# A transformer kernel on one Trainium2 core: modulation weights through the weight ring in three groups, feed-forward residual added on VectorE

## What is computed

```python
x = x + gla_mixer(rms_norm(x, norm1))
x = x + conv_ffn(rms_norm(x, norm2), w_up, conv_w, conv_b, w_down)
x = rms_norm(x, final_norm)

mod = silu(c) @ w_ada + b_ada                  # 1024 x 6144
sh1, sc1, gt1, sh2, sc2, gt2 = split(mod, 6)
h = x * (1.0 + sc1) + sh1
y = token_mixer(h, ...)
x = layer_norm(alpha * x + (1.0 + gt1) * y, ...)
h = x * (1.0 + sc2) + sh2
y = hier_moe(h, ...)                           # 32 experts, 2 per token
x = layer_norm(alpha * x + (1.0 + gt2) * y, ...)
```

## Time and profile before

| | |
|---|---|
| runs | 1503.31, 1504.61, 1504.91 us |
| profiled execution: its own time | 1502.36 us |
| its span, first to last instruction | 1500.6 us |
| mean granted TensorE clock | 0.929 |
| busy: TensorE / VectorE / ScalarE | 1238.5 / 382.4 / 248.2 us |
| moved by DMA | 332.73 MB, mean 222 GB/s |

### The profile page before, as it was taken

One profiled execution on the slowest core, in us unless ns is written; L12 is line 12 of the kernel. 1 busy time (PEld: TensorE's weight loads), 2 busy tenths in 40 slices (PEclk: granted clock), 3 DMA queues, 4 the chain that ended last, 5 costly groups with the idle time before them and its releaser, 6 DMA issues.

```text
span 1500.6 us, 21760 instructions
## 1 busy us (share of the span) xinstructions
PE 1238.5 (83%) x8810; PEld 855.2 (57%) x8811; DVE 382.4 (25%) x898; ACT 248.2 (17%) x519; POOL 31.9 (2%) x12
## 2 busy tenths in 40 slices
PE   6997899999969999999799999577757547776773
PEld 4644477777747778878579886343323224443331
DVE  1103121121121714332524211422211121222123
ACT  1311011111110111352121100211111111111112
POOL 0000000000000000000322000000000000000000
PEclk9999999999998999999999899879988889988787
DMA  8442366766722354233030046659999999899993
GB/s 302 160 144 86 119 199 225 260 199 228 253 105 84 102 207 154 73 138 126 19 113 1 1 151 220 224 203 395 393 394 395 393 394 395 305 393 393 396 393 135
DMA packets 184258, 332.73 MB, mean 222 GB/s; under 512 B 8961, under 2 KB 55169, under 8 KB 184082
## 3 DMA queue, kind: packets, MB, share of 16 engines
q1 hardware_dynamic: 184210, 332.04, 61.3%
HBM read 330.97 MB, written 1.05 MB: 221 GB/s over the span
## 4 chain that ended last, share of the span: by engine, by line
PE 65%; SPq 18%; DMA 5%; DVE 5%; ACT 3%; issue 3%; PEldq 1%; PEld 1%; DVEq 0%; ACTq 0%
SPq L428 18%; PE ps L481 17%; PE ps L598 10%; PE ps L489 9%; PE ps L607 5%; DMA main<-in_w_up 4%; PE ps L998 3%; PE ps L616 2%; PE ps L863 1%; PE ps L868 1%; PE ps L988 1%; PE ps L1013 1%; PE ps L867 1%; PE ps L768 1%; PE ps L473 1%
## 5 line engine op out<-in xcount | busy, mean ns | idle before, releaser
L998 PE MATMUL ps<-main 128*32 128x256 f32 x2176 | 165.8, 470 | 144.4 <-DMA main<-in_w_up 116.8
L481 PE MATMUL ps<-main 128*128 128x256 f32 x1152 | 252.6, 381 | 1.3 <-DVE main L1345 1.3
L481 PEld LDWEIGHTS ps<-main 128*128 128x128 f32 x1152 | 219.4, 191 | 33.9 <-issue 2.6
L998 PEld LDWEIGHTS ps<-main 128*32 128x32 f32 x2176 | 84.9, 134 | 225.4 <-DMA main<-in_w_up 126.5
L598 PE MATMUL ps<-main 128*128 128x256 f32 x704 | 155.4, 379 | 0.0
L598 PEld LDWEIGHTS ps<-main 128*128 128x128 f32 x704 | 133.0, 190 | 25.2 <-issue 8.1
L489 PE MATMUL ps<-main 128*128 128x512 f32 x320 | 138.3, 593 | 4.3 <-DVE main L1577 2.6
L489 PEld LDWEIGHTS ps<-main 128*128 128x128 f32 x320 | 60.5, 190 | 79.6 <-issue 74.6
L1406 DVE SCALAR_TENSOR_TENSOR main<-ps,cols,main 128x255 f32<-128x255 f32 (+1 forms) x88 | 38.4, 478 | 188.1 <-ACT main L1129 185.2
L1771 DVE TENSOR_TENSOR main<-main,ps 64x256 f32<-64x256 f32 x34 | 14.4, 423 | 270.8 <-ACT main L1286 270.8
L607 PE MATMUL ps<-main 128*128 128x512 f32 x176 | 81.0, 603 | 0.0
(11 more groups left out here) (307 smaller groups left out, 1095.2 us busy)
## 6 DMA issues: line engine op xcount, KB each, us to landing
main<-in_w_up SPq DMA_DIRECT2D x32, 2048.0 KB, 22.1
main<-in_w_down SPq DMA_DIRECT2D x32, 2048.0 KB, 19.5
main<-in_w_gate SPq DMA_DIRECT2D x32, 2048.0 KB, 19.1
main<-in_w_in SPq DMA_DIRECT2D x15, 2048.0 KB, 7.6
main<-in_w_ada SPq DMA_DIRECT2D x12, 2048.0 KB, 9.6
main<-in_l_ffn_w_up SPq DMA_DIRECT2D x44, 512.0 KB, 5.2
main<-in_l_gla_w_in SPq DMA_DIRECT2D x6, 2048.0 KB, 13.1
main<-in_l_ffn_w_down SPq DMA_DIRECT2D x22, 512.0 KB, 6.8
```

Source lines behind the costliest of these rows:

```text
L481: m = pe.matmul(ps[:, banks[m4 // 2], (m4 % 2) * T:(m4 % 2) * T + T], chunk8(n)[:, k, m4 * P:(m4 + 1) * P], act[:, k, :], start=(k == 0), ...
L998: m = pe.matmul(ps[q * SLOTS:(q + 1) * SLOTS, 5, 0:T], xsel[s][:, k, :], w, start=(k == 0), stop=(k == KD - 1))
```

## The change

`w_ada`'s 12 chunks become ring chunks, in three groups of four. Group 0 takes numbers 6 to 9, the output projection 10 and 11 (`C_GO`), groups 1 and 2 numbers 12 to 19; the second block begins at 20. Group 0's matmuls stand between the attention's last matmul and the transposes of its output, group 1's between the output projection and the transposes of the second norm, group 2's between the last `ff_down` and the third norm's transposes. A group fills one PSUM bank, ScalarE copies it as a whole (`take_ada`), TensorE transposes it in four pieces, VectorE adds bias and, where needed, 1, in two operations. The feed-forward loses the modulation work and the matmuls with the identity; its first `ff_down` starts the sum, and VectorE adds x at the end. The silu of the condition moves to the beginning.

```diff
         for i in range(6):
             add_chunk(wide(w_gla, HALF * i))
-        for i in range(2):
-            add_chunk(wide(I["l0_gla_w_out"], HALF * i))
+        C_ADA = [add_ada(0)]
+        C_GO = [add_chunk(wide(I["l0_gla_w_out"], HALF * i)) for i in range(2)]
+        C_ADA += [add_ada(1), add_ada(2)]
         N_FIRST = len(CHUNKS)
...
-            for n in range(N_FIRST):
+            for n in range(6):
                 load_ring(sp, n)
...
-            sp.wait_ge(S["y_turned"], 4)
-            load_ada(0)
-            for n in range(N_FIRST, N_FIRST + RING):
+            for n in range(6, N_FIRST):
                 load_ring(sp, n)
             with sp.Fori(1, FT // 2) as i:
 
                 load_up(i * 2, 0, i * 2 - 1)
                 load_up(i * 2 + 1, 1, i * 2)
-                load_ada(i, i)
                 load_down(i * 2, 0, i * 2 - 1)
                 load_down(i * 2 + 1, 1, i * 2)
-            load_ada(11, 11)
...
-            for n in range(N_FIRST + RING, N_SECOND):
+            for n in range(N_FIRST, N_SECOND):
                 load_ring(sp, n)
...
+            def ada(group, b):
+
+                for a, n in enumerate(C_ADA[group]):
+                    ring_wait(pe, n)
+                    for k in range(KD):
+                        for q in range(4):
+                            m = pe.matmul(ps[q * 32:(q + 1) * 32, b, a * P:(a + 1) * P], cond[:, k:k + 1].broadcast_to([P, 32]),
+                                          chunk8(n)[:, k, q * P:(q + 1) * P], start=(k == 0), stop=(k == KD - 1), skip_group_check=True)
+                    m.then_inc(S["chunk_done"], 1)
+
+            def ada_turn(group, b):
+
+                pe.wait_ge(S["ada_rows_ready"], group + 1)
+                for a in range(4):
+                    m = pe.transpose(ps[:, b, a * P:(a + 1) * P], ada_rows[:, a * P:(a + 1) * P], ident)
+                m.then_inc(S["ada_turned"], 1)
+
+            pe.wait_ge(S["cond_ready"], 1)
+            ada(0, 6)
             pe.wait_ge(S["y_ready"], 2)
+            pe.wait_ge(S["ada_rows_ready"], 1)
             turn_rows(y_rows, (0, 1, 5, 6), "y_turned")
...
+            ada_turn(0, 1)
+            ada(1, 0)
             pe.wait_ge(S["rows_scaled"], 4)
             turn_rows(xn, (4, 5, 6, 7), "turned")
-            for j in range(NT):
-                for half in range(2):
-                    pe.matmul(ps[:, 2 * j + half, :], ident, x[:, j, half * HALF:(half + 1) * HALF], start=True, stop=False)
             pe.wait_ge(S["turned_copied"], 8)
...
             ff_up(0, 0, (None,))
             ff_up(1, 1, (None,))
-            pe.wait_ge(S["cond_ready"], 1)
-            ada(16)
-            ff_down(1, 16, 0)
-            ada_turn(1)
+            ada_turn(1, 7)
+            pe.wait_ge(S["mod_ready"], 1)
+            ff_down(1, 16, 0, first=True)
             with pe.Fori(1, FT // 2) as i:
                 ff_up(i * 2, 0, (i * 2 - 1, i * 32 + 32))
                 ff_down(i * 2, i * 16, 1)
                 ff_up(i * 2 + 1, 1, (i * 2, i * 32 + 32))
-                ada(i * 16 + 16)
                 ff_down(i * 2 + 1, i * 16 + 16, 0)
-                ada_turn(i + 1, i)
-            ada(16 * 12)
             ff_down(FT, 16 * (FT // 2), 1, last=True)
-            ada_turn(12, 11)
+            ada(2, 6)
...
+            pe.wait_ge(S["ada_rows_ready"], 3)
             turn_k(x, "x_turned")
...
             m.then_inc(S["chunk_done"], 1)
+            ada_turn(2, 3)
             ring_wait(pe, C_KW)
...
             norm_root(0, [x[:, j, :] for j in range(NT)], NT)
+            act.wait_ge(S["cols_loaded"], 16)
+            act.activation(cond, col("cond"), ACT.Silu).then_inc(S["cond_ready"], 1)
...
+            def take_ada(group, b):
+
+                act.wait_ge(S["chunk_done"], C_ADA[group][3] + 1)
+                if group:
+                    act.wait_ge(S["ada_turned"], group)
+                act.activation(ada_rows, bank(b), ACT.Copy).then_inc(S["ada_rows_ready"], 1)
...
+            modulation(0, 1, 0)
+            ff_conv(0, 0, 0, 2)
+            ff_mul(0, 0, None)
+            modulation(1, 7, 8)
...
-                    if s == 0:
-                        modulation(i - 1, i)
-                take_ada(i + 1)
-            modulation(10, 11)
-            take_ada(12)
-            modulation(11, 12)
             dve.wait_ge(S["down_done"], FT)
-            dve.tensor_copy(unit(0), bank(0, 4)).then_inc(S["x2_ready"], 1)
+            dve.tensor_tensor(unit(0), unit(0), bank(0, 4), ALU.add).then_inc(S["x2_ready"], 1)
...
-            dve.wait_ge(S["mod_ready"], 12)
-            dve.tensor_scalar(mod[:, 8:24], mod[:, 8:24], 1.0, None, ALU.add).then_inc(S["mod_plus"], 1)
-            dve.tensor_scalar(mod[:, 32:48], mod[:, 32:48], 1.0, None, ALU.add).then_inc(S["mod_plus"], 1)
-            dve.wait_ge(S["mod_plus"], 2)
+            dve.wait_ge(S["mod_ready"], 2)
...
```

More of the change, by code:

```diff
@@ L176, in build_program, with add_ada @@
         w_gla = I["l0_gla_w_in"]
+        w_ada = I["w_ada_2"].rearrange("b d n -> (b d) n")
+        def add_ada(group):
+            return [add_chunk(wide(w_ada, HALF * (4 * group + i))) for i in range(4)]
         for i in range(6):
             add_chunk(wide(w_gla, HALF * i))
-        for i in range(2):
-            add_chunk(wide(I["l0_gla_w_out"], HALF * i))
+        C_ADA = [add_ada(0)]
+        C_GO = [add_chunk(wide(I["l0_gla_w_out"], HALF * i)) for i in range(2)]
+        C_ADA += [add_ada(1), add_ada(2)]
         N_FIRST = len(CHUNKS)
@@ L241, in build_program @@
         ident = const("ident")
[L245 to L246 removed]
+        ada_rows = unit(10, 0, HALF)
         mod = small[:, 32:80]
@@ L600, in ff_up, with ff_down @@
                 m.then_inc(S["up_done"], 1)
-            def ff_down(done, loaded, s, last=False):
+            def ff_down(done, loaded, s, first=False, last=False):
                 pe.wait_ge(S["hm_ready"], done)
@@ L607, in ff_down @@
                         m = pe.matmul(ps[:, 2 * j + half, :], hm[s][:, j * P:(j + 1) * P],
-                                      down_w[s][:, half * HALF:(half + 1) * HALF], start=False, stop=last)
+                                      down_w[s][:, half * HALF:(half + 1) * HALF], start=first, stop=last)
                 m.then_inc(S["down_done"], 1)
[L611 to L625, removed]
             ff_up(0, 0, (None,))
             ff_up(1, 1, (None,))
-            pe.wait_ge(S["cond_ready"], 1)
-            ada(16)
-            ff_down(1, 16, 0)
-            ada_turn(1)
+            ada_turn(1, 7)
+            pe.wait_ge(S["mod_ready"], 1)
+            ff_down(1, 16, 0, first=True)
             with pe.Fori(1, FT // 2) as i:
@@ L687, in _ @@
             pe.wait_ge(S["widx_ready"], 1)
+            pe.wait_ge(S["mod_ready"], 3)
             project_cols(C_QA[0], (2, 3), act=h1T)
@@ L1142, in _ @@
             norm_root(3, [x[:, j, :] for j in range(NT)], NT)
-            act.wait_ge(S["mod_plus"], 2)
+            take_ada(2, 6)
+            act.wait_ge(S["mod_ready"], 2)
             for k in range(4):
@@ L1392, in _ @@
             for half, banks in ((0, (2, 4)), (1, (3, 7))):
-                dve.wait_ge(S["chunk_done"], 7 + half)
+                dve.wait_ge(S["chunk_done"], C_GO[half] + 1)
                 for j in range(NT):
@@ L1419, in ff_mul, with modulation @@
                 dve.tensor_tensor(hm[s], sig[s], conv[s][:, 1, :], ALU.mult).then_inc(S["hm_ready"], 1)
-            def take_ada(done):
-                dve.wait_ge(S["ada_done"], done)
-                dve.tensor_copy(ada_rows, ps[:, 6, 0:P]).then_inc(S["ada_rows_ready"], 1)
-            def modulation(i, done):
-                dve.wait_ge(S["ada_turned"], done)
-                dve.tensor_tensor(mod[:, bass.ds(i * 4, 4)], ps[:, 7, 0:P].rearrange("p (q r) -> p q r", q=4)[:, :, 0], cols[:, bass.ds(COLS["b_ada"][0] + i * 4, 4)], ALU.add).then_inc(S["mod_ready"], 1)
-            for i in range(2):
-                ff_conv(i, i, i, 2 * i + 2)
-                ff_mul(i, i, None)
-            take_ada(1)
+            def modulation(group, b, plain):
+                dve.wait_ge(S["ada_turned"], group + 1)
+                turned = bank(b).rearrange("p (n r) -> p n r", n=16)[:, :, 0]
+                bias = col("b_ada")[:, 16 * group:16 * group + 16]
+                for n0 in (0, 8):
+                    m = dve.scalar_tensor_tensor(out=mod[:, 16 * group + n0:16 * group + n0 + 8], in0=turned[:, n0:n0 + 8],
+                                                 scalar=0.0 if n0 == plain else 1.0, in1=bias[:, n0:n0 + 8], op0=ALU.add, op1=ALU.add)
+                m.then_inc(S["mod_ready"], 1)
+            modulation(0, 1, 0)
+            ff_conv(0, 0, 0, 2)
+            ff_mul(0, 0, None)
+            modulation(1, 7, 8)
+            ff_conv(1, 1, 1, 4)
+            ff_mul(1, 1, None)
             with dve.Fori(1, FT // 2) as i:
@@ L1465, in _ @@
             dve.tensor_scalar(widx, ps[:, 2, 0:2 * IH], INDEX_SCALE, None, ALU.mult).then_inc(S["widx_ready"], 1)
```

(1 more changed line is left out.)

16 lines of the change are left out of this document (8 added, 8 removed).

## The result

| | before | after |
|---|---|---|
| median | 1504.76 us (1503.31 to 1505.05, 4 runs) | 1599.43 us (1599.06 to 1602.31, 4 runs) |
| ratio, 95% interval | | 1.0635 [1.0617, 1.0654] |
| span of the profiled execution | 1500.6 us | 1597.3 us |
| mean granted clock | 0.929 | 0.899 |

The kernel became 6.4% slower: 94.7 us, where 32.5 us of gain were predicted. TensorE's busy time hardly changed (1238.5 before, 1253.5 after), so the loss is waiting. The question is where.

What follows compares the result with a forecast made beforehand. TensorE was taken to bound the feed-forward, with everything behind moving along. Residual add 30.0 us earlier, plus 3.1 of clock, minus 0.5 for transposes, taken as 32.5: profiled 1502.36 to 1469.9, median 1472.1 us, range 1467 to 1482.

Steps and rivals of the forecast that it cites:

- First norm: Before the attention's output projection: group 0's chunks fill TensorE's idle time at full clock; projection ends 0.6 us earlier.
- Second norm: Before the feed-forward: group 1's fourth chunk lands late, a 1.5 us wait; up projections still start 2.0 us earlier.
- Entry: Into the feed-forward loop: up weights queue behind chunks 16 to 19, 0.5 us stall; loop starts at 199.55, 2.9 earlier.
- the case of late weights: Rival, chance 0.12: loads behind the second norm come later than counted, giving 1474.5 us, or 1477 if 5 us late.
- Loop: Feed-forward loop: a turn falls from 22.87 to 20.88 us without modulation matmuls and a transpose, 19.9 us over ten turns.
- End and third norm: Behind the feed-forward loop: 0.7 us wait, residual add 30.0 us earlier; kept clock gains 3.1, four transposes cost 0.5.
- the sum: Whole kernel: 30.0 + 3.1 - 0.5 = 32.6, taken as 32.5 us of gain.
- The DMA stream: Loads behind the second norm: counted at 410 GB/s; by the skill's 358 GB/s the time would be 1475.6 us.
- The step that failed: Everything behind the feed-forward, experts included, moves earlier with it as a block; expert loop of unchanged length.
- my rivals: Late weights 0.12, modulation stretches losing the clock 0.08, gain absorbed by experts' weights 0.02, load-bound feed-forward 0.02, more clock 0.04.
- The one for a slower kernel: Rival, chance 0.02: the feed-forward becomes bound by its loads; at 14 us a turn, 1508 us.
- the number on record: Forecast median of the whole changed kernel: 1472.1 us.

Runs made afterwards that it cites:

- 128 drains: Changed kernel with 128 drain instructions, which compute nothing, at the start of TensorE's program, moving its code: 1469.19 us, ratio 0.9785 to the kernel before.
- with 96: Kernel before with 96 drain instructions, which compute nothing, at the start of TensorE's program: 1503.33 us, ratio 1.0004.
- 112 drains: Kernel before with 112 drain instructions, which compute nothing, at the start of TensorE's program: 1500.67 us, ratio 0.9997.
- 32 drains: Changed kernel with 32 drain instructions, which compute nothing, at the start of TensorE's program: 1473.67 us, ratio 0.9825 to the kernel before.
- the eight starts in the table: Expert-loop starts 41 to 233 in TensorE's program, set by drains in either kernel; 169 and 185 gave 1599.43 to 1634.74 us, the others 1468.86 to 1503.33.
- the residual alone: Kernel before with only the identity matmuls taken out and x added on VectorE, modulation left as it was: 1504.17 us, ratio 1.0017.

## Why the prediction was wrong

The steps, with the trace of the changed kernel, and with 128 drains beside it where it differs. One thing comes ahead of them. The attention's last matmuls, before which nothing on TensorE was changed, start at 126.58 us before, 127.90 after and 124.44 with 128 drains; the kernel before with 96 and with 112 drains has them at 124.55 and 128.40. That is how one execution differs from another, so times are compared as distances from these matmuls.

- *First norm.* The chunks filled the gap and the clock stayed up. From the attention's last matmuls to the projection it took 13.31 us instead of 14.28, a gain of 1.0 where 0.6 was counted. With 128 drains it took 13.30.
- *Second norm.* The fourth chunk was late, as worked out, and by more: a wait of 3.19 us instead of 1.5. It landed 9.2 us after the projection's end (168.78 to 177.95), where the shortest landing of a ring load, 7.6, was counted. With 128 drains the wait was 1.41 us, but a wait on issue of 1.58 stood ahead of it, and the chunk was just as late (165.31 to 174.57).
- *Entry.* Predicted 199.55, which is 73.0 us after the attention's last matmuls. It took 75.60 us as it stands (203.50) and 75.51 with 128 drains (199.95), against 75.87 before. So the entry gained 0.3 us and not 2.9: the case of late weights happened, at 2.6 us, at both starts of the loop. As it stands, the first up projections behind the stall also took 8.86 us instead of 7.07, at a clock of 0.80.
- *Loop.* 20.68 us a turn, predicted 20.88. Ten turns gave 21.9 us instead of 19.9.
- *End and third norm.* The wait of 0.75 for the product was predicted at 0.7. x2's add takes 2.29 us, the copy's price. The C_CKV projection took 7.17 us (predicted 7.07): the clock was kept. From the attention's last matmuls to its end it took 308.56 us as it stands and 308.69 with 128 drains, against 339.01 before: 30.4 us gained, where the sum has 32.5. The absolute times (433.13 with 128 drains against the 465.59 of the earlier trace rows) give 32.5 to the digit, but by luck: 2.1 of it is an execution that was ahead from the start.
- *The DMA stream.* From chunk 15's landing to the up weights the working had 23.9 us at the 410 GB/s of the earlier trace rows. The estimate from the figure of 358 GB/s in the Trainium skill (DMA: Bandwidth & Descriptors, section Bandwidth) had 26.7. Measured were 25.55 us as it stands (177.95 to 203.50) and 25.38 with 128 drains (174.57 to 199.95): between the two. The DMA engines moved 387 GB/s from 178 to 190 us, and 349 from 190 to 203, where the 512-byte rows of the up weights come in.

**The step that failed** is the first one: "I take everything behind the feed-forward as a block that moves with it." What it rested on held: the experts' loads are released by compute, and the block did move, by 28.1 us. But its own length was put at no change, without a reason, and it was not the same any more. Its loop starts at another place in TensorE's program, touches eight pieces instead of seven, and runs from refetched instructions: 125.8 us lost (1599.43 against 1473.67 with 32 drains), against 33 to 35 us gained. The working costed each added instruction by its time on the engine and never by its room in the program. None of my rivals was this one. The one for a slower kernel sought the loss in the feed-forward's loads, and the feed-forward is not bound by them at all (turns of 20.68 us, TensorE at work for 201.52 of the 204 us from 200 to 404).

The sum itself came out within what the runs can tell: 33.6 us (27 to 38) at an equal start, 32.5 predicted, and at 1469.19 us the kernel with 128 drains is 2.9 us below the number on record. Within the sum the entry was counted 2.6 us too well and the loop 2.0 us too badly, so part of the agreement is luck.

What the profile of before could have told: the earlier trace rows show a loop at 0.87 clock that waits for loads, and section 3 of the page shows 37 pieces for a program of 37.4, so not one piece fetched twice in a loop of ten turns. A loop of 6.1 pieces can touch seven or eight of them, and a change that writes out 1,152 instructions ahead of it decides anew which.

## What to carry to other kernels

When a change adds or removes instructions ahead of a long loop, read the number of pieces on the instruction queue before and after: if it exceeds the length of the program, a loop is being fetched anew, and the waits on "issue" are its price. Where a wait on "issue" cuts a run of equal matmuls, a piece begins; count from there how many pieces the loop touches. Before a slower result is put down to a change, try it with some drains ahead of the loop; here 32 of them turned 6.4% slower into 1.8% faster. And when the gain of a change is to be measured, compare the two kernels at the same start, since a few instructions can outweigh it three times.

## What the runs showed of the hardware

- TensorE keeps a loop of 1,567 instructions (6.1 pieces of 16 KB) after its first turn while it touches seven pieces: at six of the eight starts in the table, and at that of the residual alone, no piece is fetched again. At the two starts where it touches eight, nine are fetched in each turn.
- The pieces are fetched one ahead. With 128 drains a fetch begins at 170.3 us, and the wait that ends at 172.65 is at the first instruction of a piece. The next fetch, at 177.0, is long after that, and TensorE comes to the next piece only at about 190 us. Seven pieces and the one ahead are eight, and eight and the one ahead are the nine that are fetched in each bad turn. The Trainium skill, Runtime: NRT & Kernel Launch, section Instruction fetch mechanics, gives TensorE 128 KiB, eight such pieces, and says that a taken branch whose target is outside the current window of two pages forces a fetch. The traces agree with the first statement, not with the second: at the good places the branch back jumps over six pieces in each turn and fetches nothing. Loops of other lengths weren't run, so eight pieces as the size of the store is a reading, not a measurement. The loop also jumps over the code for experts with more tokens three times a turn, about one piece each time; what these jumps add was not tried.
- A refetched piece costs about 2.0 us with the DMA engines nearly idle, and 3.0 us beside a full stream of weights. Straight code is not free of such waits either: in the changed kernel with 128 drains two of the runs of 256 modulation matmul records are cut, by 1.58 us at 172.65 and by 1.35 us at 419.92. By the count in the program both cuts lie where a piece begins, at 194 and 195, four pieces of 256 apart within one instruction:

```profile
172.65 0.51 PE L581 MATMUL ps<-main,small 128*32 128x128 f32 x9 [1.58 <-issue]
```

```profile
419.92 0.41 PE L581 MATMUL ps<-main,small 128*32 128x128 f32 x3 [1.35 <-issue]
```

- Such waits also take clock: in the loop (1020 to 1470 us) it fell from 0.87 to 0.79 with the same matmuls.
